# A mixture-of-experts decode step on one core: output projections in three passes, w_o before the sample rows, and other row loads moved

## The reference, cut to what matters

```python
mod = silu(c) @ w_ada + b_ada              # shift1, scale1, gate1, shift2, scale2, gate2: one row per sequence
u = x * (1 + scale1) + shift1
b_g, c_g, xa, xp, g_a, g_b = split(u @ w_in)
y_a = (b_g * conv(c_g * xa)) @ w_out_a     # 512 -> 1024
y_b = (pool(xp) @ w_pool * ls_pool) @ w_out_b   # 512 -> 1024
merged = sigmoid(g_a) * y_a + sigmoid(g_b) * y_b
h = layer_norm(ALPHA * x + gate1 * (merged @ w_o), ln1_g, ln1_b)
v = h * (1 + scale2) + shift2
f = moe_ffn(v)                             # top 4 of 32 experts, clamped SwiGLU, 1024 -> 2048 -> 1024
y = layer_norm(ALPHA * h + gate2 * f, ln2_g, ln2_b)
```

## Time and profile before

| | |
|---|---|
| median of 3 runs | 1286.19 us (1282.35 to 1286.59) |
| the profiled execution | 1285.98 us, its span 1284.2 us |
| PE busy | 1203.0 us, 94% of the span |
| DVE / ACT / POOL busy | 564.1 / 259.1 / 135.5 us |
| DMA | 466.34 MB, mean 363 GB/s |
| granted PE clock, mean | 0.976 |
| chain that ended last | PE 64%, DMA 26%, DVE 5% |

### The profile page before, as it was taken

One profiled execution on the slowest core, in us unless ns is written; L12 is line 12 of the kernel. 1 busy time (PEld: TensorE's weight loads), 2 busy tenths in 40 slices (PEclk: granted clock), 3 DMA queues, 4 the chain that ended last, 5 costly groups with the idle time before them and its releaser, 6 DMA issues.

```text
span 1284.2 us, 17106 instructions
## 1 busy us (share of the span) xinstructions
PE 1203.0 (94%) x5978; PEld 521.6 (41%) x5979; DVE 564.1 (44%) x1080; ACT 259.1 (20%) x409; POOL 135.5 (11%) x84
## 2 busy tenths in 40 slices
PE   5999999989999999989999999999999999999992
PEld 2588886633333333333333333333333333333330
DVE  0506915864443343333443343443343443343466
ACT  1523210342121211111121211111211111211111
POOL 0456452034300000000000000000000000000000
PEclk9999999969999999999999999999999999999996
DMA  9866697369999999999996999998899999699971
GB/s 337 326 248 263 246 306 247 108 266 420 408 427 426 427 426 427 425 425 426 426 419 260 425 425 426 427 427 355 321 427 427 426 427 426 288 388 429 425 325 41
DMA packets 54861, 466.34 MB, mean 363 GB/s; under 512 B 5527, under 2 KB 5687, under 8 KB 18713
## 3 DMA queue, kind: packets, MB, share of 16 engines
q1 hardware_dynamic: 53257, 461.42, 87.4%
q0 software_dynamic: 1584, 4.66, 1.1%
HBM read 464.29 MB, written 1.77 MB: 363 GB/s over the span
## 4 chain that ended last, share of the span: by engine, by line
PE 64%; DMA 26%; DVE 5%; ACT 2%; issue 1%; POOL 1%; SPq 0%; DVEq 0%; ACTq 0%; POOLq 0%
PE bank L904 26%; DMA ring<-in_w_up 24%; PE bank L938 13%; PE bank L689 8%; PE bank L882 3%; PE bank L740 3%; PE bank L804 2%; PE bank L757 2%; DMA ring<-in_w_ada 2%; PE bank L675 1%; PE bank L631 1%; PE bank L929 1%; ACT front L1104 1%; POOL front L565 1%; DVE front L1459 1%
## 5 line engine op out<-in xcount | busy, mean ns | idle before, releaser
L904 PE MATMUL bank<-ring,front 128*64 128x512 f32 x2240 | 506.7, 598 | 21.5 <-DMA ring<-in_w_up 21.5
L904 PEld LDWEIGHTS bank<-ring,front 128*64 128x64 f32 x2240 | 153.3, 137 | 316.7 <-issue 270.4
L938 PE MATMUL bank<-ring,front 128*64 128x512 f32 x1120 | 251.3, 602 | 7.2 <-ACT front L1104 7.2
L1412 DVE TENSOR_TENSOR front<-front,bank 128x512 f32<-128x512 f32 (+1 forms) x210 | 143.9, 685 | 58.9 <-PE bank L882 33.0
L1371 DVE TENSOR_TENSOR O_parts<-bank,O_parts 64x512 fp32r<-64x512 f32 x70 | 48.2, 688 | 239.9 <-ACT O_parts L1064 235.6
L938 PEld LDWEIGHTS bank<-ring,front 128*64 128x64 f32 x1120 | 78.0, 138 | 156.4 <-issue 142.5
L1101 ACT ACTIVATE front<-front 128x256 f32<-128x256 f32 x70 | 29.2, 417 | 505.1 <-DVE front L1450 505.1
L1450 DVE TENSOR_SCALAR front<-bank 128x256 f32<-128x256 f32 x70 | 29.7, 425 | 159.4 <-PE bank L904 158.1
L1064 ACT ACTIVATE O_parts<-bank 64x512 fp32r<-64x512 f32 x70 | 41.4, 592 | 238.6 <-PE bank L938 237.7
L882 PE MATMUL bank<-O_parts,onehot_T 128*128 128x512 f32 x214 | 78.9, 448 | 3.8 <-DVE front L1498 2.0
L518 POOL TENSOR_TENSOR ring_parts<-ring,ring_parts 128x1024 fp32r<-128x1024 f32 x28 | 68.0, 2461 | 81.6 <-ACT ring_parts L977 81.6
(11 more groups left out here) (229 smaller groups left out, 829.1 us busy)
## 6 DMA issues: line engine op xcount, KB each, us to landing
ring<-in_w_up SPq DMA_DIRECT2D x128, 2048.0 KB, 18.4
ring<-in_w_down SPq DMA_DIRECT2D x128, 1024.0 KB, 17.7
ring<-in_w_ada SPq DMA_DIRECT2D x12, 2048.0 KB, 11.9
ring<-in_w_in SPq DMA_DIRECT2D x7, 2048.0 KB, 7.8
ring<-in_w_o SPq DMA_DIRECT2D x2, 2048.0 KB, 21.2
hx<-in_x_prompt SPq DMA_DIRECT2D x2, 1024.0 KB, 8.4
ring<-in_w_in SPq DMA_DIRECT2D x4, 512.0 KB, 22.3
ring<-in_w_out_a SPq DMA_DIRECT2D x1, 2048.0 KB, 7.4
```

Source lines behind the costliest of these rows:

```text
L904: last = mm(bank[B_UP[j]][64 * h:64 * h + 64, :], x_T[:, (c % 2) * 2 + b, 64 * (c // 2):64 * (c // 2) + 64], w[:, :, at:at + 256], start=F ...
L938: last = mm(bank[B_DOWN][64 * h:64 * h + 64, :], act_T[:, 2 * j + b, 64 * hh:64 * hh + 64], expert_chunk_at(UP_CHUNKS + m)[:, b * 1024 + h ...
L1412: signal(TT(Y[0:r, 2 * t + h, :], Y[0:r, 2 * t + h, :], bank[b][0:r, :], ALU.add), bank_free[b], value)
```

## The change

**The output projections.** `out` now computes w_out_a and w_out_b as the w_in chunks are: ACT makes the high parts of two more chunks (`SPLIT_N`, into slots 2 and 3) and of the two inputs (eight copies of 128x320), POOL makes the low parts of the weights, DVE those of the inputs, and PE does 3 x 4 matmuls per block in fp32r. Since slots 2 and 3 are taken longer, the second w_o chunk goes to slot 0, both w_o chunks wait for `out_a7`, and the first expert's chunks change slots.

**The rows.** SP asks for the prompt rows, then both w_o chunks, then the sample rows. ln1_g and ln1_b for h are loaded once `out_b7` is done. gate2's rows are asked for as soon as v's parts exist. h is made one tile a round. ln2_g and ln2_b are asked for when the last expert's weights have landed. The subtractions for b_up's parts stay on POOL, its copies move to ACT.

The diff, cut to its core (`FRONT_SLOT` and `EXPERT_SLOT` change one slot each; regions shift by 4 elements):

```diff
+SPLIT_N = IN_N + (OUTA_N, OUTB_N)
...
-EXPERT_SLOT = (0, 4, 2, 3, 5, 1)
+EXPERT_SLOT = (3, 4, 2, 0, 5, 1)
...
+        y_parts = [[nc.alloc_sbuf_tensor_at(f"{name}_{part}", [P, 4, NT], F32R, offset=start + 4 * (RING * CH + at))
+                    for part, at in (("high", high), ("low", low))] for name, high, low in (("y_in", 8296, 9576), ("yg", 2560, 10856))]
...
-            for i in range(1, 8):
-                slot = front_slot(IN_N[i])
+            def low_of_weights(i):
+
+                slot = front_slot(SPLIT_N[i])
...
+            for i in range(1, 9):
+                low_of_weights(i)
...
-            part(pool.memset(b_up_parts, 0.0))
-            pool.wait_ge(bias_landed, 48)
-            part(pool.tensor_copy(b_up_parts[0:96, :], b_up_rows[0:96, :]))
-            for q in (1, 2):
+            pool.memset(b_up_parts, 0.0).then_inc(b_up_sub, 1)
+            low_of_weights(9)
+            for n, q in enumerate((1, 2, 2)):
                 rows, parts = b_up_rows[32 * q:32 * q + E, :], b_up_parts[32 * q:32 * q + E, :]
...
+                pool.tensor_tensor(rows, rows, parts, ALU.subtract).then_inc(b_up_sub, 1)
+
+            wait_full(pool, "out_b7")
+            pool.dma_start(norm1_rows[:, 0, :], a["ln1_g"][0].partition_broadcast(P)).then_inc(norm1_again, 16)
+            pool.dma_start(norm1_rows[:, 1, :], a["ln1_b"][0].partition_broadcast(P)).then_inc(norm1_again, 16)
...
                 pool.wait_ge(row_normed, i + 1)
+                pool.wait_ge(onehot_ready, i + 3)
...
             pool.wait_ge(h_ready, 3)
+            pool.wait_ge(expert_landed[EXPERT_CHUNKS - 1], 16 * E)
+            pool.dma_start(tail_rows[:, 2 * D:3 * D], a["ln2_g"][0].partition_broadcast(P)).then_inc(norm2_landed, 16)
+            pool.dma_start(tail_rows[:, 3 * D:], a["ln2_b"][0].partition_broadcast(P)).then_inc(norm2_landed, 16)
...
+            def out(i, name, y):
+
+                weights = lambda slot: ring_parts[:, slot, :].rearrange("p (k m) -> p k m", k=4)
+                high, low = weights(HIGH_SLOT[i % 2]), weights(front_slot(SPLIT_N[i]))
+                pe.wait_ge(w_high_ready, 4 * i)
+                pe.wait_ge(y_low_ready, 4 * (i - 7))
+                passes = ((high, y[0]), (high, y[1]), (low, y[0]))
+                for m in range(8):
                     ps = take(f"{name}{m}")
...
-                if i + 2 < 8:
+                if i + 2 < 10:
                     split_high(i + 2)
...
+            for n, (y, (high, low)) in enumerate(zip((y_in_T, yg_T), y_parts)):
+                for k in range(4):
+                    dve.wait_ge(y_high_ready, 4 * n + k + 1)
+                    signal(TT(low[:, k, :], y[:, k, :], high[:, k, :].bitcast(F32), ALU.subtract), y_low_ready, 4 * n + k + 1)
...
-            dve.wait_ge(norm1_landed, 16 * (3 + NSEQ))
+            dve.wait_ge(norm1_landed, 16 * 3)
             gain_and_offset(0)
             residual(0, 0)
+            dve.wait_ge(sample1_landed, 16 * NSEQ)
             gain_and_offset(1)
...
+                if t == 0:
+                    dve.wait_ge(norm2_landed, 32)
```

More of the change, by code:

```diff
@@ L163, in program @@
         pool_s = region(front, 7556, 4, NSEQ, HIST_P + TSEQ)
[L164 to L169, removed]
+        diff_T = region(front, 8296, 4, NT)
+        y_in_T = region(front, 9576, 4, NT)
+        yg_T = region(front, 10856, 4, NT)
+        ga_T = region(front, 12136, KC, NT)
+        gb_T = region(front, 14696, KC, NT)
+        sum_p = region(front, 17256, 2, HIST_P + NP_TOK)
         sum_s = region(front, 17800, 2, NSEQ, HIST_P + TSEQ)
@@ L384, in front_chunk @@
                 s = front_slot(n)
-                if n in O_N:
-                    wait_chunk_read(sp, IN_N[6 + O_N.index(n)])
+                if n == O_N[0]:
+                    wait_full(sp, "out_a7")
                 if len(in_slot(n)) > 1:
@@ L480, in _ @@
                     sp.wait_ge(v_ready, 6)
+                elif s == HIGH_SLOT[1]:
+                    wait_full(sp, "out_b7")
                 else:
@@ L565, in _ @@
                 pool.tensor_tensor(V[0:r, t, :], V[0:r, t, :], v_parts[0:r, PART_AT[t][q], :], ALU.subtract).then_inc(v_rest_ready, 1)
-            pool.wait_ge(b_up_ready, 1)
-            pool.dma_start(norm1_rows[:, 0, :], a["ln1_g"][0].partition_broadcast(P)).then_inc(norm1_again, 16)
-            pool.dma_start(norm1_rows[:, 1, :], a["ln1_b"][0].partition_broadcast(P)).then_inc(norm1_again, 16)
+            pool.wait_ge(v_part_ready, len(PARTS))
+            pool.dma_start(tail_rows[:, 0:D], mod_rows[0, 5 * D:].partition_broadcast(P)).then_inc(tail_landed, 16)
+            for s in range(NSEQ):
+                pool.dma_start(tail_rows[TSEQ * s:TSEQ * (s + 1), D:2 * D],
+                               mod_rows[1 + s, 5 * D:].partition_broadcast(TSEQ)).then_inc(tail_landed, 16)
             pool.wait_ge(norm1_again, 32)
@@ L579, in _ @@
                 pool.tensor_scalar(row, row, ALPHA, 1.0, ALU.mult, ALU.mult).then_inc(h_ready, 1)
-            pool.wait_ge(v_part_ready, len(PARTS))
             pool.wait_ge(h_ready, 3)
[L582 to L586, removed]
-            pool.dma_start(tail_rows[:, 3 * D:], a["ln2_b"][0].partition_broadcast(P)).then_inc(tail_landed, 16)
+            pool.wait_ge(expert_landed[EXPERT_CHUNKS - 1], 16 * E)
+            pool.dma_start(tail_rows[:, 2 * D:3 * D], a["ln2_g"][0].partition_broadcast(P)).then_inc(norm2_landed, 16)
+            pool.dma_start(tail_rows[:, 3 * D:], a["ln2_b"][0].partition_broadcast(P)).then_inc(norm2_landed, 16)
             pool.wait_ge(out_stored, 16 * 4)
@@ L734, in _ @@
                     pool_and_states()
-            def out(name, w, y, ms):
-                for m in ms:
-                    ps = take(f"{name}{m}")
-                    for k in range(4):
-                        last = mm(ps[:, 0:NT], w[:, k, m * P:(m + 1) * P], y[:, k, :], start=k == 0, stop=k == 3)
-                    done(f"{name}{m}", last)
-            pe.wait_ge(conv_ready, 4)
-            out("out_a", chunk(OUTA_N).rearrange("p (k m) -> p k m", k=4), y_in_T, range(8))
-            for g in range(4):
-                wait_read(pe, f"pool{g}")
-            out("out_b", chunk(OUTB_N).rearrange("p (k m) -> p k m", k=4), yg_T, range(8))
+            def out(i, name, y):
[5 more added lines that the diff above has]
+                for m in range(8):
+                    ps = take(f"{name}{m}")
+                    for n, (w, rhs) in enumerate(passes):
+                        for k in range(4):
+                            if m == 0 and n == 2:
+                                pe.wait_ge(w_low_ready, 4 * (i - 1) + k + 1)
+                            last = mm(ps[:, 0:NT], w[:, k, m * P:(m + 1) * P], rhs[:, k, :], start=n == 0 and k == 0, stop=n == 2 and k == 3)
+                    done(f"{name}{m}", last)
+            out(8, "out_a", y_parts[0])
+            out(9, "out_b", y_parts[1])
             wo = [chunk(n).rearrange("p (k m) -> p k m", k=4) for n in O_N]
@@ L1013, in _ @@
                         free(name, AF(state_rows[0:r, n, :], ps[0:r, :], ACT.Copy))
+                    wait_full(act, "pool3")
+                    for k in range(4):
+                        act.wait_ge(conv_ready, k + 1)
+                        AF(y_parts[0][0][:, k, :], y_in_T[:, k, :], ACT.Copy).then_inc(y_high_ready, 1)
+                    for k in range(4):
+                        wait_read(act, f"pool{k}")
+                        AF(y_parts[1][0][:, k, :], yg_T[:, k, :], ACT.Copy).then_inc(y_high_ready, 1)
+            act.wait_ge(bias_landed, 48)
+            act.wait_ge(b_up_sub, 1)
+            AF(b_up_parts[0:3 * E, :], b_up_rows[0:3 * E, :], ACT.Copy).then_inc(b_up_copied, 1)
+            for n, q in enumerate((1, 2, 2)):
+                act.wait_ge(b_up_sub, n + 2)
+                AF(b_up_parts[32 * q:32 * q + E, :], b_up_rows[32 * q:32 * q + E, :], ACT.Copy).then_inc(b_up_copied, 1)
             def root(n, r):
```

57 lines of the change are left out of this document (31 added, 26 removed).

## The result

The changed kernel takes 1279.12 us (median of 8 runs, 1275.79 to 1282.75) against 1285.78 us (8 runs of the kernel before): ratio 0.9948, 95% interval 0.9934 to 0.9962, or 6.7 us less. The profiled execution has a span of 1277.5 us against 1284.2 us, which is 6.7 us too, so the two traces can be set side by side. The forecast was 9.5 us less, which is outside the 4.9 to 8.5 us that the interval leaves.

A forecast was written before the change was run, and what follows sets the result against it. PE bounds the front up to T0, the DMA engines from there to 666 us, then PE again. 4.0 us (T0) and 5.5 us (DMA) off 1285.98 us gave 1276.5 us, range 1271 to 1283.5.

The forecast's parts named there:

- The projections: w_out_a and w_out_b in three passes: 28.54 us instead of 34.65, PE gains 6.1 us, inputs ready in time.
- w_o: Both chunks wait for out_a7 at 192.7 us, land near 209 us; PE waits 2 us, the gain is 4.1 us.
- the case for 203.5 us: Bound at w_o: if sample DMAs were the slow part, w_o is there at 203.5 us, gain the full 6.1 us.
- T0: End of the front, PE having used the second expert's first chunk, 279.19 us: 4.0 us sooner, sign at about 275 us.
- The row vectors: ln1 and ln2 rows, 2.1 MB, leave the DMA-bound part after T0: 5.5 us less while the queue stays full.
- h: One tile a round: saves PE up to 4 us before 437 us, costed at 0, keeps a DMA hole under 1 us closed.
- The end: ln2's rows, asked for at 1245 us, land by about 1255 us, before ACT reads them from 1259 us: costs nothing.
- Rival 1: w_o late: T0 0 to 3 us later than before, only the DMA term stays, say 1282 us; chance 0.14.
- Rival 2: After T0, removed bytes are not the bound, holes open up and only T0 counts: 1282 us; chance 0.10.
- Rival 3: T0 and DMA gains both at their upper ends, 6.1 + 6.4 = 12.5 us: 1273.5 us; chance 0.13.
- Rival 4: Slower: sample rows land last and hold DVE, v's rows, the router and T0 wait: 1289.5 us; chance 0.06.
- Rival 5: In out's projections a missing part makes each block wait, PE's 6.1 us are lost: 1280.5 us; chance 0.05.

The follow-up runs named there:

- The filled wait: The changed kernel with three float32 matmuls on constants between out_b and w_o, in place of PE's 2.3 us wait: 1278.48 us, ratio 0.9938 against the kernel before.
- the run with the rows sooner: The changed kernel with ln1's rows and x asked for ahead of the modulation store, ACT's copy for it ahead of w_out_b's high parts: 1273.49 us, ratio 0.9905.

## Why the prediction came out as it did

**Direction and range were right. The size, 9.5 us for 6.7, was too large by a term that was 2 us off, and one step's price was wrong without showing in the sum.**

- *The projections.* 28.54 us worked out, 28.33 measured. Their inputs were ready as said. One cover was thinner than I wrote: DVE's gate step also has an operation with both inputs in SBUF (L1282, 128x320), and beside POOL's 4.1 us subtraction for b_up one of them took 3.97 us instead of 0.49. PE's 28.33 us show no wait for it.

```profile
200.56 3.97 DVE L1282 TENSOR_TENSOR front<-front 128x320 f32<-128x320 f32 x1
```

- *w_o.* Landing and wait were right (2 us said, 2.28 measured), in part by luck. The sum as written gives 198 + 9.8 = 207.8 us for the landing, a wait of 0.8 us and a gain of 5.3; the step from there to "near 209" has no reason given, and the case for 203.5 us (192.7 + 9.8 = 202.5) has the same 1 us in it. The step that failed is "Then PE waits 2 us and the gain is 4.1 us": it left out what the wait does to the clock. With the clock's 1.94 us the gain at the end of w_o is 6.32 - 2.28 - 1.94 = 2.1 us (at T0 100.78 - 98.45 = 2.3 us), not 4. The T0 that was named as a sign, about 275 us, came at 278.84: 1.98 us by the late start of out_a, the rest by this. The filled wait shows that the standstill is the cause, the run with the rows sooner what it was worth (4.2 of its 4.6 us). The trace before had shown the clock at 0.50 in the router from 255 to 275 us, where PE waits in bits, and I didn't carry that over to a new wait.
- *The row vectors.* 5.5 us said, 5.77 measured. ln2's pair back in the stretch cost 2.69 us; ln1's pair was not run by itself with h out of the way.
- *The sample rows.* With them ahead of w_o PE waited 7.9 us longer, about 6 us of it theirs. By the Trainium skill ("DMA: Bandwidth & Descriptors", section on why a DMA increments its semaphore by 16) an 8-partition DMA runs on 8 engines; my estimate from that rule is double the time, 3.7 us for 0.8 MB. The measurement goes further than that estimate, and says nothing of the engines one by one. They were part of what was slow in the earlier trace rows, and not all of it: from 195 to 200 us the engines moved 274 GB/s with the sample rows ahead and 405 without, but the rows that still stood ahead of w_o went at only 288 GB/s from 185 to 195 us, and w_o didn't land by 203.5 us as the prediction's bound for that case had it.
- *h.* Costed at 0, with "a hole of under 1 us" if left out. The sum came out because h was spread. The price was wrong: the load of ln1's rows was what held h back, and taking it away moves h into the first round's activation, where it costs a hole of some 7 us in the queue and makes the stretch 3.8 us longer instead of 5.5 shorter; the 2 us that the hole doesn't cover are not explained. I had followed where h was, and not where it would go once its input came sooner. Of my reason for spreading it, only that it must not meet an activation is left.
- *The end.* Nothing, as said; the landing took 4.2 and 4.8 us, less than the 6.7 to 9.2 taken as bound.
- *The rivals.* Rival 1 (w_o late) happened in part; that ln1's rows share the engines with a late w_o was seen only with the sample rows ahead of it (0.72 MB before it landed). Rival 2 needs holes, and none were there. Rival 3 needed the full 6.1 us in front. Rival 4 had the sample rows late behind w_o, and DVE didn't wait for them. Late w_o alone can undo the change: with the sample rows ahead of it PE's wait reaches 10.2 us, and everything the change brings is gone (0.9998). Rival 5 didn't happen, by the 28.33 us.

**What stays open.** Why out_a starts within a spread of 4.4 us, which hides gains of this size in single runs. Why the stretch was 401.44 us with the rows and h moved but plain projections, and 399.77 us with the three passes; T0 came late against the first w_down there (T0 + 19.6). And what sets the time from the end of w_o to T0: it was between 29.4 and 31.4 us in the 13 profiles, 31.4 in the kernel before, 31.2 in the changed kernel and 29.7 with the filled wait. So a comparison from out_a to T0 is good to about 2 us. Up to the end of w_o it is much closer: 69.37 us in all three profiles with plain projections, 67.2 to 67.7 with the 2.3 to 2.8 us wait, 66.1 with the wait filled, and 63.05 to 63.07 in the four with the rows sooner.

## What to carry to other kernels

A new wait of 2 us on TensorE cost 4 us here, since its clock fell behind it: count both, and look first for an idle stretch of the DMA engines from which the awaited load can start sooner. When a load is moved forward, follow whatever it had been holding back: a GpSimd step that is released early can land beside the VectorE work of the critical path. In a stretch that the DMA queue sets, 1.05 MB cost 2.7 us here and moving row vectors out pays, but only while the queue stays full behind it: 0.8 MB taken from just before a place where it runs thin brought 0.85 us in one pair of runs and nothing in another.

## What the runs showed that I had not expected

- A standstill of 2.28 us on TensorE at full clock was followed by pieces of w_o that took 1.94 us longer (15.67 for 13.73), although the clock fell only after TensorE had resumed, and one of 10.2 us by 3.15 us (16.88). With matmuls on constants in its place there was 0.24 us.
- Sixteen DMAs of 8 partitions with 0.8 MB in all, put ahead of 4.2 MB, made TensorE's wait 7.9 us longer, of which another queue's 0.72 MB took about 1.8 us.
- POOL at work on SBUF held back DVE operations with two SBUF inputs: four of 0.42 to 0.68 us took 2.35 to 2.62 us beside POOL operations of about 2.4 us, and one of 0.49 us took 3.97 us beside one of 4.1 us. They lasted about as long as POOL's operation and not as long as their own size asks. The operation just ahead of the last, with one input in PSUM, kept its 0.49 us beside the same POOL operation.
